# A two-layer hybrid decoder trunk: scan placed behind its rotation, wider GpSimd operations, the gate channels in column groups, and another order at both ends of the mixer

## The reference

```python
h = x + 0.5 * swiglu(rms_norm(x, ffn1_norm), ffn1_w_in, ffn1_w_out)      # d_ff 2816
u = rms_norm(h, mix_norm)
sb_qkv, s5_u, gq, gk, gv, gr, gg, dsa_qkv, gates = split(u @ w_in)
y_sb  = stick_breaking_attention(sb_q, sb_k, sb_v)                       # 4 heads of 64
y_s5  = s5_mixer(s5_u, ...)       # bu = B u; state[t] = lam_bar * state[t-1] + bu[t]; y = Re(C state); GLU
y_gla = gla_mixer(gq, gk, gv, gr, gg, w_gate, b_gate, norm)              # z = gg @ w_gate + b_gate, gg has 16 channels
y_dsa = dilated_mixer(d_q, d_k, d_v, ...)                                # norm, rope, softmax
per_branch = einsum('bsnw,nwd->bsnd', stack(y_sb, y_s5, y_gla, y_dsa), w_branch)
h = h + sum_n(sigmoid(gates) * per_branch) @ w_out
h = h + 0.5 * swiglu(rms_norm(h, ffn2_norm), ffn2_w_in, ffn2_w_out)
```

## Time and profile before

| | |
|---|---|
| Time, median of 3 runs | 1290.23 us (1284.02 to 1292.07) |
| The profiled execution, its own time | 1289.22 us |
| its span | 1287.3 us |
| mean granted TensorE clock | 0.992 |
| busy: TensorE, VectorE, ScalarE, GpSimd | 97%, 70%, 50%, 25% of the span |
| HBM read | 218.42 MB, 170 GB/s over the span |

### The profile page before, as it was taken

The page is one execution under the profiler, slowest core; times in us unless marked ns, Lnnn a source line. Parts: engine busy times, 40 slices in busy tenths (PEclk is TensorE's granted clock), DMA queues, the critical chain, the costliest instruction groups (busy, mean ns, idle before and its releaser), DMA issues.

```text
span 1287.3 us, 25597 instructions
## 1 busy us (share of the span) xinstructions
PE 1245.8 (97%) x10328; PEld 1222.4 (95%) x10328; DVE 895.5 (70%) x1172; ACT 640.0 (50%) x904; POOL 327.4 (25%) x462
## 2 busy tenths in 40 slices
PE   5999999999999999999999999999999999999998
PEld 5999999888999999999999999998889999999998
DVE  4766857877877676555676687687887786656554
ACT  5654545663544454444456445557625444534432
POOL 0388800364003300000005895005630041000000
PEclk9999999998999999999999999999999999999999
DMA  7555554542344365555545545544333454555541
GB/s 299 199 185 174 180 179 165 175 149 99 131 158 166 135 236 198 191 195 168 191 135 201 188 165 200 189 164 152 135 130 131 154 186 160 201 184 175 186 173 66
DMA packets 31029, 220.46 MB, mean 171 GB/s; under 512 B 3568, under 2 KB 3568, under 8 KB 4592
## 3 DMA queue, kind: packets, MB, share of 16 engines
q1 hardware_dynamic: 30960, 219.49, 49.0%
HBM read 218.42 MB, written 1.05 MB: 170 GB/s over the span
## 4 chain that ended last, share of the span: by engine, by line
PE 75%; DVE 12%; POOL 7%; ACT 3%; issue 2%; DMA 0%; DVEq 0%; SPq 0%; ACTq 0%
PE banks L456 24%; PE banks L457 24%; PE banks L458 24%; DVE w_lo_t L1072 5%; PE banks L469 3%; ACT w_hi_t L812 1%; POOL st L1631 1%; DVE s5x L1274 1%; POOL s5x L1629 1%; POOL s5x L1628 1%; POOL st L1634 1%; POOL st L1536 1%; POOL st L1632 1%; DVE u_lo_t L1084 1%; DVE hT L1223 1%
## 5 line engine op out<-in xcount | busy, mean ns | idle before, releaser
L1072 DVE TENSOR_TENSOR w_lo_t<-raw,w_hi_t 128x1024 fp32r<-128x1024 f32 x408 | 518.0, 1310 | 107.8 <-ACT w_hi_t L812 107.4
L812 ACT ACTIVATE w_hi_t<-raw 128x1024 fp32r<-128x1024 f32 x408 | 407.2, 1046 | 126.7 <-PE banks L458 126.0
L456 PE MATMUL banks<-u_hi_t,w_hi_t 128*128 128x256 f32 x1520 | 436.0, 287 | 18.2 <-DVE w_lo_t L1072 14.1
L457 PE MATMUL banks<-u_lo_t,w_hi_t 128*128 128x256 f32 x1520 | 431.9, 284 | 0.0
L458 PE MATMUL banks<-u_hi_t,w_lo_t 128*128 128x256 f32 x1520 | 431.9, 284 | 0.0
L456 PEld LDWEIGHTS banks<-u_hi_t,w_hi_t 128*128 128x128 f32 x1520 | 293.6, 193 | 22.5 <-DVE w_lo_t L1072 14.1
L457 PEld LDWEIGHTS banks<-u_lo_t,w_hi_t 128*128 128x128 f32 x1520 | 293.8, 193 | 0.1
L458 PEld LDWEIGHTS banks<-u_hi_t,w_lo_t 128*128 128x128 f32 x1520 | 293.5, 193 | 0.0
L456 PE MATMUL banks<-b_hi_t,w_hi_t 128*128 128x256 f32 x864 | 245.1, 284 | 1.9 <-DVE b_lo_t L1084 1.9
L457 PE MATMUL banks<-b_lo_t,w_hi_t 128*128 128x256 f32 x864 | 244.5, 283 | 0.0
L458 PE MATMUL banks<-b_hi_t,w_lo_t 128*128 128x256 f32 x864 | 244.5, 283 | 0.0
(11 more groups left out here) (215 smaller groups left out, 1267.7 us busy)
## 6 DMA issues: line engine op xcount, KB each, us to landing
raw<-weights SPq DMA_DIRECT2D x203, 1024.0 KB, 4.9
prm<-params SPq DMA_DIRECT2D x1, 1178.5 KB, 5.3
prm<-params SPq DMA_DIRECT2D x1, 1166.5 KB, 15.1
cst<-constants SPq DMA_DIRECT2D x1, 1027.0 KB, 11.1
hT<-x_t SPq DMA_DIRECT2D x2, 512.0 KB, 5.5
raw<-weights SPq DMA_DIRECT2D x2, 512.0 KB, 6.4
out_t<-hT SPq DMA_DIRECT2D x4, 256.0 KB, 2.2
prm<-params SPq DMA_DIRECT2D x1, 12.0 KB, 1.9
```

The lines of the kernel that those rows point to most:

```text
L456: pe.matmul(o, st[0], mv[0], start=start, stop=False, skip_group_check=True)
L457: pe.matmul(o, st[0], mv[1], start=False, stop=False, skip_group_check=True)
L812: act.activation(w_hi[:, slot, a:a + HALF], raw[:, slot, a:a + HALF], ACT.Copy) \
L1072: dve.tensor_tensor(w_lo[:, slot, a:a + HALF], raw[:, slot, a:a + HALF], w_hi[:, slot, a:a + HALF].bitcast(F32), ALU.subtract).then_inc(s. ...
```

## The change

- `gg` is no longer a block. Its 16 weight columns per k-tile lie in `prm` (`w_gg`), and TensorE computes the channels in `pieces(1)` with 16 plain-fp32 matmuls (`gate_channels`), four at a time in the four column groups of 32; the sum over the groups is made by `w_gate`, which now has 128 rows. VectorE multiplies with the row of rstd in its `pieces(1)`. All later positions of `SEQ` move up by one, and some change places: (0, 1) stands before gv, and (1, 2), (1, 3) before (0, 2), (0, 3). The numbers in `pieces` stay as they were.
- The output projection has six blocks instead of five: (4, 5) is split into (4) and (5). The count of blocks stays at 36.
- VectorE scans directly after it rotates, at the same position. GpSimd works on both tiles of a pair at once: six operations of 128 x 512.
- At position 22, which is now gate block (3, 0) right ahead of `out0`, VectorE does its pieces (`b_lo` of branches 2 and 3) before the rest of the weights. TensorE waits at `out0` for three of the four `b_lo`, and for the fourth ahead of the first matmul of branch 3.
- At `out3` VectorE does both gates before the rest of the weights, and ScalarE rounds the next block before it makes the sums 6 and 7 hi.
- x and the first block come in quarters, each with its own semaphore; ScalarE does one small activation before x has landed; TensorE waits for each quarter of the rest of the first block.
- The constant of minus ones is one column, broadcast where it is used.

The diff, cut to these parts:

```diff
-SEQ = ["s5u", "sbq", "sbk", "gg", "gqk", "dq", "dk", (0, 0), "sbv", "gv", (0, 1), "dv", "gr", (1, 0), (1, 1),
-       (0, 2), (0, 3), (1, 2), (1, 3), (2, 0), (2, 1), (2, 2), (2, 3),
+SEQ = ["s5u", "sbq", "sbk", "gqk", "dq", "dk", (0, 0), "sbv", (0, 1), "gv", "dv", "gr", (1, 0), (1, 1),
+       (1, 2), (1, 3), (0, 2), (0, 3), (2, 0), (2, 1), (2, 2), (2, 3),
        (3, 0), "out0", (3, 1), "out1", (3, 2), "out2", (3, 3), "out3"]
 NSEQ = len(SEQ)
 NBRANCH = 4
-OUT_TILES = [(0, 1), (2, 3), (4, 5), (6,), (7,)]
+OUT_TILES = [(0, 1), (2, 3), (4,), (5,), (6,), (7,)]
...
-MIXED_AT = [((0,), (1,)), ((), ()), ((), ()), ((2, 3, 4, 5, 6), (7,))]
+MIXED_AT = [((0,), (1,)), ((), ()), ((), ()), ((2, 3, 4, 5), (6, 7))]
...
-            sp.dma_start(hT[:, 0:4, :], x_in[:, 0:4, :]).then_inc(s_x[0], 16)
-            sp.dma_start(raw[:, 0, 0:HALF], stream[0][:, 0:HALF]).then_inc(s_first, 16)
-            sp.dma_start(hT[:, 4:8, :], x_in[:, 4:8, :]).then_inc(s_x[1], 16)
-            sp.dma_start(raw[:, 0, HALF:BLK], stream[0][:, HALF:BLK]).then_inc(landed[0], 16)
+            for q in range(4):
+                a = QUARTER * q
+                sp.dma_start(hT[:, 2 * q:2 * q + 2, :], x_in[:, 2 * q:2 * q + 2, :]).then_inc(s_x[q], 16)
+                sp.dma_start(raw[:, 0, a:a + QUARTER], stream[0][:, a:a + QUARTER]) \
+                    .then_inc(s_first[q] if q < 3 else landed[0], 16)
...
+                        if layer == 0 and norm == 0 and j == 0:
+                            if q % 2 == 0:
+                                pe.wait_ge(s.q_lo, q // 2 + 1)
+                            else:
+                                pe.wait_ge(s.w_lo, 2 * RING + (q + 1) // 2)
+                        elif q == 0:
                             block_ready(b + j)
...
+                    def gate_channels():
+                        for n, (part, half) in enumerate(itertools.product(range(2), range(2))):
+                            for j in range(4):
+                                kt = 4 * half + j
+                                a = PARAM["w_gg"][0] + 16 * kt
+                                ins = single(banks[32 * j:32 * j + 32, 2, T:2 * T], prm[:, a:a + 32],
+                                             u_hi[:, kt, :].bitcast(F32) if part == 0 else u_lo[:, kt, :].bitcast(F32),
+                                             n == 0, n == 3)
+                        ins.then_inc(s.gg, 1)
                     def pieces(m):
+                        if m == 1:
+                            gate_channels()
                         if m in S5_AT:
                             s5_in(S5_AT.index(m))
...
-                            pe.wait_ge(s.evac_v, layer * PER.evac_v + NTH[SLOT["gg"]])
-                            single(banks[:, 2, 0:T], p_("w_gate")[0:16, :], gq[0:16, :]).then_inc(s.gla_z, 1)
+                            pe.wait_ge(s.gg_evac, layer * PER.gg_evac + 1)
+                            single(banks[:, 2, 0:T], p_("w_gate"), gq[:, :]).then_inc(s.gla_z, 1)
...
-                            pe.wait_ge(s.b_lo, layer * PER.b_lo + 4)
+                            pe.wait_ge(s.b_lo, layer * PER.b_lo + 3)
                             pe.wait_ge(s.y, layer * PER.y + 2)
                         for dt in range(2):
                             if q >= 1:
                                 pe.wait_ge(s.gated, layer * PER.gated + 2 * (q - 1) + dt + 1)
                             for n in range(4):
+                                if (q, dt, n) == (0, 0, 3):
+                                    pe.wait_ge(s.b_lo, layer * PER.b_lo + 4)
...
+            act.activation(nrm[:, 0, :], prm[:, 0:2], ACT.Copy)
+            act.wait_ge(s.w_used, 1)
+            for q in range(4):
+                split_pair(0, "g_ffn1", q)
+                act.wait_ge(s_first[q] if q < 3 else landed[0], 16)
+                a = QUARTER * q
+                act.activation(w_hi[:, 0, a:a + QUARTER], raw[:, 0, a:a + QUARTER], ACT.Copy) \
+                    .then_inc(s.q_hi if q % 2 == 0 else s.w_hi, 1)
...
+                    if m == 1:
+                        dve.wait_ge(s.gg, layer * PER.gg + 1)
+                        dve.tensor_tensor(gq[:, :], banks[:, 2, T:2 * T], rstd_row[:, :], ALU.mult) \
+                            .then_inc(s.gg_evac, 1)
...
                     if m in S5_AT:
                         s5_rotate(S5_AT.index(m))
-                    if m - 1 in S5_AT:
-                        s5_scan(S5_AT.index(m - 1))
+                        s5_scan(S5_AT.index(m))
...
                             q = int(SEQ[m][3])
+                            gate(2 * q)
                             if q == 3:
                                 for dt in range(2, 6):
                                     mixed_lo(dt)
-                            gate(2 * q)
+                                gate(2 * q + 1)
                             rest_of_weights(layer, k0 + m // RING + 1, m % RING)
-                            gate(2 * q + 1)
+                            if q < 3:
+                                gate(2 * q + 1)
                             continue
                         if not BY_ACT[m]:
                             evacuate(m)
+                        if m == 22:
+                            pieces(m)
                         rest_of_weights(layer, k0 + m // RING + 1, m % RING)
                         if m == SLOT["out0"] + 1:
                             mixed_lo(0)
                             mixed_lo(1)
-                        pieces(m)
+                        if m != 22:
...
-                        if o != 3:
+                        if tiles[-1] % 2 == 1:
...
-                        if o < 4:
+                        if o < 5:
                             rest_of_weights(layer, k0 + m // RING + 1, m % RING)
-                        if o in (2, 4):
+                        if o in (3, 5):
...
-                    for i in range(2):
-                        t = 2 * pair + i
-                        own.mark(pool.tensor_tensor(x[:, i, 0, 0, :], x[:, i, 1, 0, :], rotC[:, t, :], ALU.mult))
-                        own.mark(pool.tensor_tensor(x[:, i, 0, 1, :], x[:, i, 1, 1, :], rotC[:, t, :], ALU.mult))
-                        re, im = st[:, i, 0, :], st[:, i, 1, :]
-                        own.mark(pool.tensor_tensor(re, x[:, i, 1, 1, :], rotS[:, t, :], ALU.mult))
-                        own.link(pool.tensor_tensor(im, x[:, i, 1, 0, :], rotS[:, t, :], ALU.mult))
-                        tt(re, x[:, i, 0, 0, :], re, ALU.subtract)
-                        pool.tensor_tensor(im, x[:, i, 0, 1, :], im, ALU.add).then_inc(s.s5_state, 1)
+                    cos, sin = (x[:, 2 * pair:2 * pair + 2, :] for x in (rotC, rotS))
+                    scan_re, scan_im = s5x[:, :, 1, 0, :], s5x[:, :, 1, 1, :]
+                    re, im = st[:, :, 0, :], st[:, :, 1, :]
+                    own.mark(pool.tensor_tensor(s5x[:, :, 0, 0, :], scan_re, cos, ALU.mult))
+                    own.mark(pool.tensor_tensor(re, scan_im, sin, ALU.mult))
+                    own.mark(pool.tensor_tensor(s5x[:, :, 0, 1, :], scan_im, cos, ALU.mult))
+                    own.link(pool.tensor_tensor(im, scan_re, sin, ALU.mult))
+                    tt(re, s5x[:, :, 0, 0, :], re, ALU.subtract)
+                    pool.tensor_tensor(im, s5x[:, :, 0, 1, :], im, ALU.add).then_inc(s.s5_state, 1)
```

106 lines of the change are left out of this document (50 added, 56 removed).

## The result

| | before | after |
|---|---|---|
| median of four runs, us | 1289.94 (1284.02 to 1292.07) | 1313.14 (1311.46 to 1313.56) |
| ratio, 95% interval | | 1.0185 (1.015 to 1.022) |
| profiled execution, us | 1289.2, span 1287.3 | 1313.56, span 1311.7 |
| time lost in the spans | | 24.4 |

The changed kernel is slower by 1.85%. The forecast had 1299.4 us and a range up to 1309: the direction of the forecast was right, the size was not, and the range missed.

The account below looks back on a forecast made before the run. The prediction took TensorE as the bound (busy 97% of the span), with VectorE the bound behind the rounding of block 10. Its terms summed to +10.2 on the profiled 1289.2 us, giving 1299.4 us, range 1275 to 1309.

Parts of the forecast that it names:

- Item 1: Gate channels: 24 matmuls go and 16 fp32 ones come at 2.1 us a layer; -1.6 us in all.
- The rival that they don't: Gate channels: column groups do not overlap four-fold, +1.6 to +5 us a layer on top of the forecast; chance 0.08.
- Item 2: Scan behind rotation, wide GpSimd: waits for states gone, -7.4 us; later masks make TensorE idle 10.0 ahead of `attend`, +15.6.
- the mask keeps up: Rival at position 12: VectorE gets there earlier, the wait of 2.2 a layer goes too; 1273 us, chance 0.2.
- half of it: Rival: no turns at the masks, +15.6 becomes +6 and +5 becomes 2; 1287 us, chance 0.15.
- Item 3: Masks before the suffix sums, positions 6 and 9: turns cause new waits at positions 7 and 10; +5.0 us.
- Item 4: Clock behind the idle time at position 12: both layers get the long half-clock stretch; +1.5 us (0 to 3).
- the slow side: Rival: same mechanism at its upper bound, +9 and +4 a layer, long half-clock stretch in both; 1308 us, chance 0.12.
- Item 5: At out0: TensorE cannot avoid waiting 1.6 us for `b_lo` of branch 2; +3.2 us (2.4 to 4).
- Item 6: Mixer's end: waits of 1.90 and 1.88 go, split blocks bring 1 to 2 us; -3.8 us (0 to -3.8).
- Item 7: The start: TensorE begins at about 7.3 instead of 14.06, then waits for the sum of squares at 18.9; -2.3 us.
- No gain at the start: One of the signs that would show the forecast wrong, where -2.3 us was predicted at the start.

Follow-up runs that it names:

- experiment 2: Changed kernel with only the fourth scan one position later, behind the masks of position 11; 1296.16 us, 1.0049 of the kernel before.
- experiment 4: Changed kernel with GpSimd's six operations of 128 x 512 a pair cut into twelve of 128 x 256; 1300.17 us, 1.0056 of before.
- experiment 5: Kernel before with one edit alone, each scan directly behind its rotation, GpSimd still narrow; 1294.93 us, 1.0019 of before.
- experiment 9: Changed kernel with softplus pieces (positions 6, 9) and masks (11) ahead of the rest of the weights, scans left behind the rotations; 1292.92 us, 1.0011.
- experiment 1: Changed kernel with all four scans one position later again, as before the change; 1291.9 us, 1.0009 of before.
- experiment 3: Changed kernel plus 76 unused matmuls in each mixer, just ahead of TensorE's wait at position 12; 1305.56 us, 1.0112 of before.
- Experiment 7: Changed kernel with scans one position later, fourth behind the rest; pieces and masks ahead of the rest, b_lo ahead of evacuation, squares ahead of rounding; 1269.1 us.

## Why the forecast was right in direction and wrong in size

**Item 1, gate channels: right.** The changed kernel's profile has them from 224.1 to 226.0, 1.9 us a layer for 2.1 predicted: the four column groups overlap. The rival that they don't is out. (Its upper end was added wrongly: 5 us a layer on top of the forecast is 1309 us, not 1306.)

**Item 2, states and mask: right.** The waits of 7.8 went, and TensorE idles 9.57 and 9.59 for 10.0. The mechanism is the one the prediction gave: scan ahead of masks, and one turn of GpSimd for each of four instructions. In its own terms, VectorE needs 16.2 us from the rest of position 10 to the end of the masks (303.00 to 319.25) where it had 17.3: 3.9 for the four turns instead of 4.6, and 2.4 for the GLA keys instead of 2.9. TensorE's way from 303.00 is 6.8 us, where 7.7 less 0.8 for the two copies was predicted. Experiments 2, 4, 5 and 9 take it apart: 3.21 left without the scan and its turns, 7.50 with narrow turns, 5.91 with the scan alone and narrow turns, 5.17 without the two halves. One part of the reasoning was superfluous: by experiment 1 the waits for the states go without the scan's move, by the wide operations and TensorE's later arrival alone. The rivals "the mask keeps up" and "half of it" are out.

**Item 3, suffix sums: right**, 3.06 for 2.5 at position 7, nothing over 0.3 at position 10.

**Item 4, the clock: the step that failed.** The prediction allowed +1.5 us (0 to 3), for one reason only: that layer 1 would have the long half-clock stretch behind `attend` that layer 0 had. It gave no clock cost to the new waits of item 3, and took the stretch of before for the longest possible. Even its own term was too small: 6.9 us more at half clock are 3.2 us at 0.46, not 1.5. The traces have 19.7 us more at half clock in the mixers; with the 0.46 from experiment 3 that is 9.1. Of it 5.2 stand behind the suffix waits (11.4 us), which the prediction had itself foreseen, and 3.8 behind `attend` (21.9 us for 13.6); a stretch behind a wait for the states went, and one at the end of layer 0 came. The numbers to see it were in the trace of before: of TensorE's seven idle times of about 2 us in the mixers (1.88 to 2.36) four had a half-clock stretch of 3.4 to 10.2 us behind them (304, 884, 940 and 1075). Each new wait should have been entered with a second price. None of the rivals gave the waits of item 3 such a price either; the slow side had 3 us for the clock in all.

**Item 5, out0: right**, 1.43 for 1.6. Experiment 7 shows that the wait was avoidable after all: with `b_lo` ahead of the evacuation of block 22 it is gone. "TensorE cannot avoid waiting" held only for the order of the change.

**Item 6, the end: half right.** The waits for `u_lo` (1.90, 1.88) are gone, and the new wait at the split blocks is there with 1.91, inside the 1 to 2 us predicted. But only -1.0 is left of -3.8 for both mixers, since the new wait takes almost all that the old one gave. The term was summed at its favourable end.

**Item 7, the start: wrong in sign.** "No gain at the start" was one of the prediction's own signs of being wrong, and it came. TensorE begins at 7.38, as predicted (7.3), and runs into the sum of squares. The prediction had that ready at 18.9, since block 1 "lands as before". It does not. ScalarE's timeline of the changed kernel:

```profile
13.98 2.01 ACT L835 ACTIVATE w_hi_t<-raw 128x1024 fp32r<-128x1024 f32 x2 [1.66 <-DMA raw<-weights]
15.89 2.17 ACT L852 ACTIVATE U<-hT 128x512 f32<-128x512 f32 x4
```

ScalarE waits for block 1 until 13.98, where it began to round it at 12.65 before. SyncE issues nine transfers ahead of it instead of five, one each 0.47 us, so block 1's is issued at 4.98 instead of 3.08 us. That alone does not explain the delay: block 1 lands 2.5 us behind the last piece of block 0 in both kernels (13.96 behind 11.47, 12.38 behind 9.89), and it is these pieces, all issued by 4.93, that land 1.6 us later as quarters. Between 6 and 8 us the DMA engines moved 176 and 188 GB/s for 393 and 291 before; why is not shown. The squares and their sum move with block 1, `sum_squares` starts at 20.32 behind an idle time of 4.44 instead of at 18.9, and 6.4 us of half clock follow (2.9 lost), where the prediction counted 1.3. In its terms: -2.9 + 1.4 + 2.9 = +1.4, of the +1.5 read. (Its own two numbers, -2.9 and +1.3, gave -1.6; it took -2.3.) Experiment 7 puts the squares ahead of the rounding: 0.63 and 1.20 of waiting instead of 4.44, and `h_lo` at 34.53, 1.4 before the kernel before. So the quarters pay once the squares don't wait for block 1.

Of the 13.4 us that the ledger's sum lies over the forecast, the clock in the mixers has 7.6, the start 3.8 and the end 2.8, less 0.8 for the others. The slow-side rival, 1308, came nearest. It gave the idle times 26 us against 20.9 read, and the clock 3 against 9.1: near in its sum, but for a reason that is not the one measured. What stays open is what sets the length of a half-clock stretch: equal idle times of 3.21 had 3.4 us behind them in one execution and 10.2 in another.

## What to carry to other kernels

When a change lets TensorE wait somewhere anew, enter the wait twice: its length, and 0.46 us for each us at half clock that may follow, unless TensorE would only run into another engine's wait there. Here the waits of 3.1 us in the changed kernel had 5.4 and 6.0 us of half-clock work behind them, those of 9.6 us 10.8 and 11.1, and of the waits of about 2 us in the kernel before some had none and one had 10.2. Where a producer is moved forward in an engine's order, look at what TensorE needs next from that same engine and put it ahead; an edit that frees one engine (GpSimd) may lose by what it pushes back on another (VectorE), and gain once the order is set right: the same parts cost 23 us in one order and gain 21 in another, with the scans' move taken back. Where two edits aim at the same wait, test whether one is enough: the wide operations had removed the waits for the states, and the scan's move on top of them only cost. When a first transfer is split, look at when what stands behind it lands: here x and block 0 had landed 1.6 us later in eight parts than in four.

## What the runs showed of the hardware that was not expected

- The turns run both ways and scale with the partner's length: beside VectorE's halves GpSimd's 128 x 512 operation took 2.25 us for 1.27, and two VectorE halves took 4.13 for 2.35; with 128 x 256 operations they took 3.05. The Trainium skill ("GPSIMD Engine Reference", section 8) says that GpSimd shares its SBUF interfaces with VectorE and contends with its instructions of two SBUF inputs; these rows agree.
- 76 matmuls whose results nobody reads, put into a wait of 9.6 us, kept the granted clock at 1.00 through the work behind it and made the kernel 7.6 us faster. It is still 9 us slower than the kernel of experiment 2, in which that wait is cut to 3.2 us.
- Sixteen fp32 matmuls of 128 rows in four column groups took 1.9 us. At 0.43 for each matmul with its fellows of the other groups that is 4 x 0.43 and a tail, full overlap of four groups; before, the trace showed two.
- One program came out between 1292.2 and 1299.8 us in eight runs (experiment 2), where the kernel of experiment 7, almost without half-clock stretches, stayed within 1.7 us in four. The changed kernel, with the most half-clock work of all, stayed within 2.1 us in four, so it is not their amount alone.
